# Moving the overflow loop of a mixture-of-experts sweep from its end to its middle

## The chip, the cores and the metric

One core of a Trainium2 chip runs the whole program. The metric is the device time of one execution in microseconds (us), a median over the runs of a kernel. The profile is one execution, taken by the hardware profiler.

## What is computed

A two-layer backbone over 512 latent tokens of width 1024, with 256 context tokens. Layer 0 mixes tokens with latent attention, layer 1 with a convolution module. After each mixer comes a mixture of experts (MoE) with 64 experts of hidden width 256, six chosen for each token, and one shared expert. All is in float32. Only the MoE matters here:

```
xs_pad = concat([xs, zeros((1, D))])
xg = xs_pad[slot_tok].reshape(n_blocks, 128, D)     # tokens grouped by expert, in blocks of 128 rows
yg = map(lambda xb, e: (silu(xb @ w1[e]) * (xb @ w3[e])) @ w2[e], (xg, blk_e))
routed = segment_sum(yg * slot_w, slot_tok)
out = routed + (silu(xs @ sh_w1) * (xs @ sh_w3)) @ sh_w2
```

How many tokens an expert gets depends on the routing. On this data most experts get 64 or fewer, some get 65 to 128, and in each layer one block of tokens lies beyond an expert's first 128.

## The kernel before

**The sweep.** `moe(i)` runs once for each layer. After routing, all engines sweep over experts u = 0 to 63, with the four blocks of the shared expert among the first ones. The w-th block of the sweep has place w; for u of 2 and more, `place(u) = u + 4`. For each expert TensorE (PE) runs `unit(u)`:

- `expert_in(u)`, the product with w1 and w3 ("up", bank 6). A flag in `big_i` picks one of two forms: `up_small` (L943, 32 matmuls, up to 64 tokens) or `up_mm` (L937, 16 matmuls). It first waits for the expert's weights (`w_in`) and its transposed rows (`xgT_ev`).
- `turn_rows(u+1)`: the next expert's gathered rows are transposed (L975, banks 1 and 2). VectorE (DVE) copies them out with `rows_out` (L1316).
- `down(u-1)`: the product of the expert before with w2 (L950 small, L964 large, banks 4 and 5).
- `turn_act(u)`: the activations are transposed (L970). DVE copies them out (L1322).

ScalarE (ACT) computes the SiLU of u (L583 small, L581 large; DVE multiplies, L1311 and L1309) and then `store(u-1)`. That copies the result out of PSUM (L609 or L607) into one of two buffers, `yb[0]` and `yb[1]`, and issues two DMAs to `y_rows` (L615). Before it overwrites a buffer it waits for that buffer's stores to land (`y_out`).

**The ring.** Weights lie in four slots of SBUF. SP, the engine that issues the weight loads, runs `refill_up` (L368, 2 MB: w1 and w3) when up has used a slot, and `refill_down` (L371, 1 MB: w2) when down has. One expert's weights are 3.15 MB, and SP keeps this order in its queue: up of u+1, then down of u.

**The rows.** GpSimd (POOL) gathers the rows of u+2 from `h_rows` by an indirect DMA (L467) as soon as the rows of u are transposed, into `xg[u % 2]`.

**The overflow loop.** Blocks beyond an expert's first 128 tokens are handled after expert 63, by a loop on every engine that runs `many` times, a count in `unit_i` that each engine loads into a register. Nothing in it overlaps: rows are gathered (L493), transposed, copied out (L1479), the up product (L937), SiLU (L652), product (L1481), transposition, copy (L1483), down product (L964), copy (L654), store of 512 KB (L656), and on ACT a wait for that store to land. Its weights go into the slot of expert 60, when expert 60's down product is done, with semaphore `t_w`.

**Combining.** When all stores have landed, POOL gathers the six results of each token (L509, 24 indirect DMAs) and DVE sums them (L1490). These lines begin it:

```
pool.wait_ge(y_out[s], 32 * E // 2 + i * 16 * E)      # for s in 0, 1
pool.wait_ge(m["dn_ps"], TT + E)
with nc.gpsimd.If(many > 0):
    pool.wait_ge(m["t_yout"], many * 16)
```

Of the kernel before, what the change touches and what calls it, by code (L numbers as in the profile page):

```python
# [26 lines left out]
E = 64  # L27
# [40 lines left out]
def build(nc, xT_d, ctxT_d, vec_d, cst_d, mod_w, wq_a, wq_b, wkv_a, wkv_b, wo, pw1, pw2,  # L68
# [10 lines left out]
    with ctx:  # L79
# [8 lines left out]
        def bank(b, n=1):  # L88
            return PS[:, b * 512:(b + n) * 512]
# [213 lines left out]
        def place(u):  # L303
            return u + 2 if u < 2 else u + 4

        def slot_of(u):
            return u if u < RING - 1 else (1, 3, 2, 0)[u % RING]

        def loads_of(u):
            return 1 if u < RING - 1 else (u - 5) // 4 + 1 if slot_of(u) == RING - 1 else (u - 2) // 4 + 1 if slot_of(u) == 2 \  # L310
                else (u - 3) // 4 + 2

# [32 lines left out]
        def _(sp):  # L345
# [12 lines left out]
            def load_moe(i):  # L358
# [34 lines left out]
                refill_up(5, RING - 1, SHARED_AT[3])  # L393
                with nc.sync.Fori(0, (E - 6) // 4) as g:
# [7 lines left out]
                sp.wait_ge(unit_rdy, i + 1)  # L402
                many = nc.sync.value_load(unit_i[0:1, XMAX:XMAX + 1], min_val=0, max_val=XMAX)
                with nc.sync.If(many > 0):
                    with nc.sync.Fori(0, many) as j:
                        sp.wait_ge(m["dn_ps"], TT + E - 3)
                        sp.wait_ge(m["t_dn"], j + 1)
                        e = nc.sync.value_load(unit_i[0:1, ds(j, 1)], min_val=0, max_val=E - 1)
                        expert(ds(e, 1), slot_of(E - 4), m["t_w"])

# [31 lines left out]
        def _(pool):  # L442
# [7 lines left out]
            def moe(i):  # L450
# [26 lines left out]
                gather(1, 1, xg_in[1])  # L477
                with nc.gpsimd.Fori(0, E // 2 - 1) as g:
# [3 lines left out]
                pool.wait_ge(xgT_ps, E - 1 + i * E)  # L482
# [52 lines left out]
        def _(a):  # L535
# [36 lines left out]
            def moe(i):  # L572
# [64 lines left out]
                shared_out(3)  # L637
                with nc.scalar.Fori(0, (E - 4) // 4) as g:
# [3 lines left out]
                either(E - 1, lambda big: silu(place(E - 1), 1, 1, big))  # L642
                either(E - 2, lambda big: store(E - 2, place(E - 2), 32 * ((E - 2) // 2), 0, big))
                either(E - 1, lambda big: store(E - 1, place(E - 1), 32 * ((E - 1) // 2), 1, big))
                a.sem_inc(m["t_yev"], 1)
                a.wait_ge(unit_rdy, i + 1)
                many = nc.scalar.value_load(unit_i[0:1, XMAX:XMAX + 1], min_val=0, max_val=XMAX)
                with nc.scalar.If(many > 0):
                    a.wait_ge(y_out[0], 32 * E // 2 + i * 16 * E)
                    with nc.scalar.Fori(0, many) as j:  # L650
# [7 lines left out]
                        a.wait_ge(m["t_yout"], j * 16 + 16)  # L658
                        A(tick[0:1, i:i + 1], zero[0:1, 0:1], ACT.Copy).then_inc(m["t_tick"], 1)

            a.wait_ge(x_in, 32)
# [104 lines left out]
        def _(pe):  # L766
# [166 lines left out]
            def moe(i):  # L933
# [166 lines left out]

                with nc.tensor.Fori(0, (E - 4) // 4) as g:
# [3 lines left out]
                unit(E - 1, slot_of(E - 1), slot_of(E - 2), 32 * loads_of(E - 1), None, 1)  # L1105
                either(E - 1, lambda big: down(place(E - 1), 1, slot_of(E - 1), big))

                many = nc.tensor.value_load(unit_i[0:1, XMAX:XMAX + 1], min_val=0, max_val=XMAX)
                with nc.tensor.If(many > 0):
                    with nc.tensor.Fori(0, many) as j:  # L1110
                        pe.wait_ge(m["t_xg"], j * 16 + 16)
                        rows_tr(0).then_inc(m["t_xgT_ps"], 1)
                        pe.wait_ge(m["t_xgT_ev"], j + 1)
                        pe.wait_ge(m["t_w"], j * 32 + 32)
                        up_mm(lambda c: xgT[0][:, c, :], slot_of(E - 4)).then_inc(m["t_up"], 1)
# [68 lines left out]
        def _(dve):  # L1184
# [114 lines left out]
            def moe(i):  # L1299
# [165 lines left out]
                weights()  # L1465
                with nc.vector.Fori(0, (E - 4) // 4) as g:
                    for r in range(4):
# [3 lines left out]
                        act_out(n, 1, (1 + r) % 2)  # L1471
                either(E - 1, lambda big: product(place(E - 1), 1, 1, big))
                act_out(place(E - 1), 1, 1)
                many = nc.vector.value_load(unit_i[0:1, XMAX:XMAX + 1], min_val=0, max_val=XMAX)
                with nc.vector.If(many > 0):
                    dve.wait_ge(m["up_ps"], TT + E - 1)
                    with nc.vector.Fori(0, many) as j:
# [3 lines left out]
                        V.tensor_tensor(act[0], gate[0], bank(6)[:, F:2 * F], ALU.mult).then_inc(m["t_act"], 1)  # L1481
                        dve.wait_ge(m["t_actT_ps"], j + 1)
                        V.tensor_copy(actT[0].rearrange("p k t -> p (k t)"), bank(7)[:, 0:F]).then_inc(m["t_actT_ev"], 1)  # L1483
                dve.wait_ge(m["y_ev"], SHARED_AT[3] + 1)
                for n in range(TT * K):
# [139 lines left out]
```

## Time and profile before

| | us |
|---|---|
| median of 3 runs | 2261.01 (2259.72 to 2262.26) |
| the profiled execution's own time | 2265.18 |
| its span, first to last instruction | 2263.4 |
| PE busy | 1923.2 (85%) |
| DVE, ACT, POOL busy | 829.7, 463.5, 346.2 |
| DMA | 624.04 MB, mean 276 GB/s |

Busy time is summed over instructions. Of PE it says little: matmuls are pipelined, and their ends are modelled. The sweep of layer 0 lies between about 584 us (up of expert 0) and 1184 us, that of layer 1 between about 1564 us and 2168 us.

### The profile page before, as it was taken

The page shows a single profiled execution, that of the slowest core. Times are in us where ns is not written, and L with a number is a line of the kernel's source. Part 1 is how long each engine was busy: PE and PEld are TensorE (multiplying, and loading weights), DVE is VectorE, ACT ScalarE, POOL GpSimd, SP SyncE. Part 2 cuts the span into 40 slices and gives each one's busy share as a digit, 9 for nine tenths or more (in the row PEclk, how much of TensorE's full clock was granted, in tenths as well). Part 3 has the DMA queues.
Part 4 walks back from the last instruction along what each step waited for, and adds up shares of the span by engine and source line. Part 5 has one row for each costly group of instructions (what it writes and reads, how often), then busy time and mean ns, then how long its engine had stood idle before and what let it go on. Part 6 is the DMA issues. An engine that isn't in the chain of part 4 may idle for free.

```text
span 2263.4 us, 30747 instructions
## 1 busy us (share of the span) xinstructions
PE 1923.2 (85%) x9400; PEld 990.9 (44%) x9401; DVE 829.7 (37%) x1481; ACT 463.5 (20%) x826; POOL 346.2 (15%) x538
## 2 busy tenths in 40 slices
PE   6999999899999878978891898788989789988952
PEld 3355555335444444444440443244444444444521
DVE  2237666405332222222225589435322212222225
ACT  4124344213011111111110455221111111110102
POOL 0000000000111111111104188001111111111122
PEclk8999999998999999999996899898999999999986
DMA  9697000567499999999987400035899999999954
GB/s 372 251 371 287 1 1 0 180 229 302 143 366 412 402 396 397 396 407 393 391 312 255 199 1 0 0 129 223 307 400 407 395 392 407 389 395 393 378 189 160
DMA packets 122815, 624.04 MB, mean 276 GB/s; under 512 B 18048, under 2 KB 19200, under 8 KB 87040
## 3 DMA queue, kind: packets, MB, share of 16 engines
q1 hardware_dynamic: 71776, 498.65, 55.8%
q0 software_dynamic: 26112, 79.72, 9.9%
q10 hardware_dynamic: 24864, 44.84, 5.6%
q8 instruction: 37, 0.61, 0.1%
q14 instruction: 26, 0.21, 0.0%
HBM read 562.34 MB, written 76.28 MB: 282 GB/s over the span
## 4 chain that ended last, share of the span: by engine, by line
PE 61%; DMA 22%; DVE 8%; issue 4%; POOL 2%; ACT 2%; SPq 0%; DVEq 0%; ACTq 0%; POOLq 0%
DMA ring<-in 19%; PE PS L937 10%; PE PS L943 9%; PE PS L1157 5%; PE PS L964 5%; PE PS L950 4%; PE PS L975 3%; PE PS L833 3%; PE PS L1175 3%; PE PS L928 2%; PE PS L862 2%; PE PS L794 2%; POOL work L509 2%; PE PS L918 2%; PE PS L785 2%
## 5 line engine op out<-in xcount | busy, mean ns | idle before, releaser
L943 PE MATMUL PS<-ring,work 128*64 128x256 f32 x3360 | 417.0, 405 | 111.1 <-issue 108.5
L943 PEld LDWEIGHTS PS<-ring,work 128*64 128x64 f32 x3360 | 248.1, 145 | 255.7 <-issue 160.6
L1311 DVE TENSOR_TENSOR work<-work,PS 64x256 f32<-64x256 f32 x105 | 44.4, 423 | 522.4 <-ACT work L583 519.2
L950 PE MATMUL PS<-ring,work 128*64 128x512 f32 x840 | 203.3, 605 | 1.4 <-ACT work L609 0.8
L937 PE MATMUL PS<-ring,work 128*128 128x512 f32 x400 | 182.3, 610 | 19.7 <-issue 13.4
L1316 DVE COPY work<-PS 128x1024 f32<-128x1024 f32 x128 | 156.7, 1224 | 14.8 <-PE PS L975 5.4
L461 POOL COPY col_i<-idx 128x1 int32 (+1 forms) x128 | 23.2, 181 | 848.9 <-PE PS L975 838.1
L467 POOL DMA_INDIRECT work<-h_rows,col_i x128 | 125.5, 981 | 169.4 <-issue 169.4
L975 PE MATMUL PS<-cst,work 128*128 128x128 f32 x1040 | 140.9, 278 | 0.6 <-DMA work<-h_rows,col_i 0.6
L583 ACT ACTIVATE work<-PS 64x256 f32<-64x256 f32 x105 | 39.4, 375 | 484.7 <-PE PS L943 484.7
L975 PEld LDWEIGHTS PS<-cst,work 128*128 128x128 f32 x1040 | 113.4, 141 | 54.2 <-issue 53.0
L937 PEld LDWEIGHTS PS<-ring,work 128*128 128x128 f32 x400 | 75.8, 195 | 110.7 <-issue 110.7
L1322 DVE COPY work<-PS 128x256 f32<-128x256 f32 x136 | 57.7, 424 | 178.3 <-PE PS L970 178.1
L964 PE MATMUL PS<-ring,work 128*128 128x512 f32 x264 | 119.2, 594 | 1.0 <-DVE work L1483 1.0
L1157 PE MATMUL PS<-hT,ring 128*128 128x512 f32 x256 | 113.3, 602 | 6.0 <-ACT hT L566 6.0
L609 ACT ACTIVATE work<-PS 128x512 f32<-128x512 f32 x105 | 62.7, 597 | 268.6 <-PE PS L950 236.0
L530 POOL TENSOR_TENSOR work<-work 128x512 f32<-128x512 f32 x80 | 104.8, 1313 | 76.5 <-ACT work L740 67.2
L881 PE MATMUL PS<-work,hT 96*128 96x512 f32 (+1 forms) x256 | 93.0, 486 | 0.0
L1127 PE MATMUL PS<-cst,work 128*128 128x128 f32 x64 | 12.2, 333 | 90.9 <-DVE work L1490 90.9
L454 POOL MEMSET work<- 128x1024 f32 x4 | 3.8, 980 | 554.4 <-DVE small L1371 554.4
L794 PE MATMUL PS<-sq,mean_w 128*128 128x512 f32 (+1 forms) x112 | 62.2, 672 | 28.4 <-ACT sq L550 25.3
L950 PEld LDWEIGHTS PS<-ring,work 128*64 128x64 f32 x840 | 51.2, 136 | 79.5 <-issue 77.5
(226 smaller groups left out, 2230.9 us busy)
## 6 DMA issues: line engine op xcount, KB each, us to landing
ring<-in SPq DMA_DIRECT2D x156, 2048.0 KB, 17.4
ring<-in SPq DMA_DIRECT2D x130, 1024.0 KB, 17.8
y_rows<-zrow POOLq DMA_DIRECT2D x2, 14336.0 KB, 70.8
y_rows<-work ACTq DMA_DIRECT2D x210, 128.0 KB, 9.1
ring<-in SPq DMA_DIRECT2D x3, 4096.0 KB, 27.5
y_rows<-work ACTq DMA_DIRECT2D x46, 256.0 KB, 9.9
ring<-in SPq DMA_DIRECT2D x1, 8192.0 KB, 25.1
ring<-in SPq DMA_DIRECT2D x2, 3072.0 KB, 12.3
```

Source lines behind the costliest of these rows:

```text
L467: pool.indirect_dma_start(out=xg[n][0:p], out_offset=None, in_=h_rows[i], in_offset=bass.IndirectOffsetOnAxis(ap=col_i[0:p, n:n + 1], axis=0),
L530: nc.gpsimd.tensor_tensor(side[c % 2], before, tap_prod[n % 4], ALU.add).then_inc(side_add, 1)
L794: mm(bank(NB)[:, 0:w], mean_w[:, :], sq[:, c % 2, 0:w], start=(c == 0), stop=(c == DC - 1)).then_inc(sq_used, 1)
L833: last = mm(bank(4 + g % 4)[0:M_, 0:w], lhs, hA[:, c, c0:c0 + w], start=(c == 0), stop=(c == DC - 1))
L881: last = mm(bank(2 * (n % 2), 2)[:, c0:c0 + w], qT[m % 2][q][0:96, t * 128:(t + 1) * 128], kT[m % 2][q][0:96, c0:c0 + w], start=True, stop ...
L937: last = mm(bank(6), lhs(c), w13(s)[:, :, c, :], start=(c == 0), stop=(c == DC - 1))
L943: last = mm(bank(6)[64 * q:64 * q + 64, 0:F], lhs(c)[:, 0:64], w13(s)[:, q, c, :], start=(c == 0), stop=(c == DC - 1), tile_position=(0, 6 ...
L950: last = mm(bank(4)[64 * q:64 * q + 64, :], actT[par][:, kk, 0:64], w2(s)[:, kk, q * 512:(q + 1) * 512], start=(kk == 0), stop=(kk == 1), ...
L964: last = mm(bank(4 + half), actT[par][:, kk, :], w2(s)[:, kk, half * 512:(half + 1) * 512], start=(kk == 0), stop=(kk == 1))
L975: last = tr(bank(1, 2)[:, c * 128:(c + 1) * 128], xg[par][:, c * 128:(c + 1) * 128], ident)
L1157: last = mm(bank(2 * (c % 2) + half), pw1_sb[:, kk, half * D + c * 128:half * D + (c + 1) * 128], hM[:, kk, :], start=(kk == 0), stop=(kk ...
L1316: V.tensor_copy(xgT[par].rearrange("p c t -> p (c t)"), bank(1, 2)).then_inc(xgT_ev, 1)
```

## The change

The overflow loop now stands between experts 38 (`MID`) and 39 on every engine.

- **Ring.** The overflow block takes one turn of the ring, as if it were an expert of its own: it gets slot 0, which expert 35 used, and each later expert the slot one turn further on. `RING_TURN`, `turn_of` and `slot_of` say so.
- **SP.** Both loads of the overflow block are issued when the down product of 35 is done, after a load of `many` and one of the expert's number. They stand ahead of the loads of 39. The refill of 42 (slot 0) waits for the overflow block's down product; behind it in SP's queue are the up load of 43 and the down load of 42.
- **POOL.** The overflow rows are gathered after the rows of 38 are transposed, and the gathers of 40 and on wait until the overflow rows are transposed.
- **PE.** The down product of 38 is no longer overlapped with the up product of 39 but comes before the overflow block. After the block PE waits for ACT's copy of its result (`t_yev`), and the unit of 39 has no down product in it.
- **ACT.** The loop first waits for the stores of `yb[0]` through expert 38 to land, then takes the SiLU. It ends in the wait for the overflow block's own store, as before; now the SiLU of 39 comes behind it.
- **DVE.** One wait is added (`dn_ps`, before the copy into `actT[0]`).
- At the end of the sweep the overflow loop is gone. The waits at the head of combining are the same.

```diff
-            return u if u < RING - 1 else (1, 3, 2, 0)[u % RING]
+            return u if u < RING - 1 else RING_TURN[turn_of(u) % RING]
...
-                for u in range((E - 6) // 4 * 4 + 5, E):
+                for u in range((MID - 6) // 4 * 4 + 5, MID + 1):
+                    if u < MID:
+                        refill_up(u + 1, slot_of(u + 1), u + 1)
+                    refill_down(u, slot_of(u), u)
+                sp.wait_ge(unit_rdy, i + 1)
+                sp.wait_ge(m["dn_ps"], place(MID - 3) + 1)
+                many = nc.sync.value_load(unit_i[0:1, XMAX:XMAX + 1], min_val=0, max_val=XMAX)
+                with nc.sync.If(many > 0):
+                    with nc.sync.Fori(0, many) as j:
+                        sp.wait_ge(m["t_dn"], j + 1)
+                        e = nc.sync.value_load(unit_i[0:1, ds(j, 1)], min_val=0, max_val=E - 1)
+                        expert(ds(e, 1), EXTRA_SLOT, m["t_w"])
+                for u in range(MID + 1, MID + 4):
+                    refill_up(u, slot_of(u), place(u - 3))
+                    refill_down(u, slot_of(u), place(u - 3))
+                with nc.sync.If(many > 0):
+                    sp.wait_ge(m["t_dn"], many + 1)
+                    sp.sem_inc(m["t_tick"], 1)
+                refill_up(MID + 4, slot_of(MID + 4), place(MID - 3))
+                refill_up(MID + 5, slot_of(MID + 5), MID + 5)
+                refill_down(MID + 4, slot_of(MID + 4), place(MID - 3))
...
+                    pool.wait_ge(m["t_xgT_ps"], many + 1)
+                    nc.gpsimd.tensor_tensor(tick[0:1, 8 * i + 5:8 * i + 6], zero[0:1, 0:1], zero[0:1, 0:1], ALU.add)
+                with nc.gpsimd.Fori(0, (E - MID - 2) // 2) as g:
+                    for r in range(2):
+                        pool.wait_ge(xgT_ps, g * 2 + (MID + 1 + r) + i * E)
+                        gather(g * 2 + (MID + 2 + r), r, xg_in[r])
...
-                    a.wait_ge(y_out[0], 32 * E // 2 + i * 16 * E)
+                    a.wait_ge(y_out[0], 32 * (MID // 2 + 1) + i * 16 * E)
...
+                either(MID, lambda big: down(place(MID), 0, slot_of(MID), big))
 
                 many = nc.tensor.value_load(unit_i[0:1, XMAX:XMAX + 1], min_val=0, max_val=XMAX)
                 with nc.tensor.If(many > 0):
+                    pe.wait_ge(xgT_ev, MID + 2 + i * E)
...
-                        pe.wait_ge(m["y_ev"], TT + E)
-                        down_mm(0, slot_of(E - 4)).then_inc(m["t_dn"], 1)
+                        pe.wait_ge(m["y_ev"], place(MID) + 1)
+                        down_mm(0, EXTRA_SLOT).then_inc(m["t_dn"], 1)
+                    pe.wait_ge(m["t_yev"], many + 1)
+
+                expert_in(MID + 1, place(MID + 1), slot_of(MID + 1), 32 * loads_of(MID + 1), 1)
+                turn_rows(MID + 2, 16 * ((MID + 2) // 2 + 1), 0)
+                turn_act(place(MID + 1), 1)
...
+                        dve.wait_ge(m["dn_ps"], place(MID) + 1)
```

The rest of the diff splits each engine's loop over experts in two, up to `MID` and from `MID + 1`, with the few units between them written out.

## Rows read from the trace of the kernel before

**Rows 1.** Stretches of time: busy us by engine, granted clock, DMA share, GB/s.

```profile
960.00:1100.00 140.00, 113.56 (x766) 60.65 (x764) 33.14 (x48) 15.25 (x32) 21.43 (x48) 0.95 1.02 400
...
1150.00:1185.00 35.00, 34.26 (x219) 18.12 (x218) 9.02 (x14) 5.61 (x10) 4.19 (x10) 1.00 0.84 299
...
1900.00:1950.00 50.00, 49.41 (x219) 25.14 (x219) 10.22 (x15) 6.17 (x10) 6.80 (x15) 1.00 1.01 396
...
1970.00:2000.00 30.00, 29.21 (x175) 15.53 (x176) 7.82 (x11) 3.73 (x7) 4.36 (x11) 0.99 0.98 378
```

**Rows 2.** Groups of PE, 964 to 1101 us: busy, mean ns, idle before.

```profile
L943 PE MATMUL PS<-ring,work 128*64 128x256 f32 x480 | 61.8, 416 | 24.5 <-issue 24.5
...
L937 PE MATMUL PS<-ring,work 128*128 128x512 f32 x1 | 1.2, 1214 | 2.4 <-issue 2.4
```

**Rows 3.** The same, 1956 to 2077 us.

```profile
L943 PE MATMUL PS<-ring,work 128*64 128x256 f32 x384 | 49.1, 414 | 14.8 <-issue 14.8
...
L937 PE MATMUL PS<-ring,work 128*128 128x512 f32 x17 | 10.0, 744 | 5.0 <-issue 5.0
```

**Rows 4.** Timeline at layer 0's end: start us, us, engine line op.

```profile
1184.22 1.09 PE L975 MATMUL PS<-cst,work 128*128 128x128 f32 x8
...
1185.36 1.12 ACTq L615 DMA_DIRECT2D y_rows<-work  x2
...
1186.72 7.13 PE L937 MATMUL PS<-ring,work 128*128 128x512 f32 x16 [1.40 <-DVE work L1479]
...
1193.89 0.38 ACT L652 ACTIVATE work<-PS 128x256 f32<-128x256 f32 x1 [8.56 <-PE PS L937]
...
1195.73 3.70 PE L964 MATMUL PS<-ring,work 128*128 128x512 f32 x8 [0.52 <-DVE work L1483]
...
1200.68 0.36 ACTq L656 DMA_DIRECT2D y_rows<-work  x1
...
1203.73 0.95 POOL L509 DMA_INDIRECT work<-y_rows,row_i  x1
```

**Rows 5.** Stores, issue to landing: L615 at the end of layer 0 (1185 to 1188 us).

```profile
DMA to landing us min/median/max: 2.3/2.3/2.4
```

**Rows 6.** The same of L656, both its executions.

```profile
DMA to landing us min/median/max: 2.6/2.6/2.7
```

**Rows 7.** Timeline at layer 1's end.

```profile
2168.77 1.14 ACTq L615 DMA_DIRECT2D y_rows<-work  x2
...
2187.35 0.96 POOL L509 DMA_INDIRECT work<-y_rows,row_i  x1
```

**Rows 8.** L368, the overflow block's 2 MB load (issued at 1169.5 us).

```profile
DMA to landing us min/median/max: 8.9/8.9/8.9
```

**Rows 9.** SP's timeline, layer 1: up load of 39, down load of 39.

```profile
1906.40 0.33 SPq L368 DMA_DIRECT2D ring<-in  x1
...
1921.20 0.33 SPq L371 DMA_DIRECT2D ring<-in  x1
```

**Rows 10.** SP's register load ahead of the overflow block's loads, ns.

```profile
L408 SPq TENSOR_LOAD <-unit_i x2: 274/278/283, 1168.8 to 2152.5; - x2
```

**Rows 11.** L371, the 1 MB load of 38 in layer 1 (issued at 1909.14 us).

```profile
DMA to landing us min/median/max: 16.1/16.1/16.1
```

**Rows 12.** PE's timeline around expert 39, layer 1.

```profile
1939.07 0.44 PE L970 MATMUL PS<-cst,work 128*128 128x128 f32 x2
...
1948.12 3.67 PE L943 MATMUL PS<-ring,work 128*64 128x256 f32 x32
```

**Rows 13.** Stores of L615, issue to landing, 1940 to 1990 us.

```profile
DMA to landing us min/median/max: 7.5/10.5/13.6
```

**Rows 14.** L371, the 1 MB load of 38 in layer 0 (issued at 929.66 us).

```profile
DMA to landing us min/median/max: 15.8/15.8/15.8
```

**Rows 15.** Stores of L615, issue to landing, 930 to 990 us.

```profile
DMA to landing us min/median/max: 8.3/10.2/13.7
```

**Rows 16.** The page's DMA issues: gathers of rows, median us to landing.

```profile
work<-h_rows,col_i POOLq DMA_INDIRECT x130, 8.9
```

More of the change, by code:

```diff
@@ L304, in place, with turn_of @@
             return u + 2 if u < 2 else u + 4
+        MID = 38
+        RING_TURN = (0, 1, 3, 2)
+        def turn_of(u):
+            return u - 3 if u <= MID else u - 2
         def slot_of(u):
-            return u if u < RING - 1 else (1, 3, 2, 0)[u % RING]
+            return u if u < RING - 1 else RING_TURN[turn_of(u) % RING]
         def loads_of(u):
-            return 1 if u < RING - 1 else (u - 5) // 4 + 1 if slot_of(u) == RING - 1 else (u - 2) // 4 + 1 if slot_of(u) == 2 \
-                else (u - 3) // 4 + 2
+            return sum(slot_of(x) == slot_of(u) for x in range(u + 1))
+        EXTRA_SLOT = RING_TURN[(MID - 2) % RING]
+        assert EXTRA_SLOT == slot_of(MID - 3)
         ROW_BANK = [n % 2 for n in range(4)] + [3, 0] * 4 + [(2, 4, 5, 6)[n % 4] for n in range(12)]
@@ L397, in load_moe @@
                         refill_down(g * 4 + (5 + r), slot_of(5 + r), g * 4 + (5 + r))
[L398 removed]
+                for u in range((MID - 6) // 4 * 4 + 5, MID + 1):
[19 more added lines that the diff above has]
+                refill_down(MID + 4, slot_of(MID + 4), place(MID - 3))
+                with nc.sync.Fori(0, (E - MID - 6) // 4) as g:
+                    for r in range(4):
+                        refill_up(g * 4 + (MID + 6 + r), slot_of(MID + 6 + r), g * 4 + (MID + 6 + r))
+                        refill_down(g * 4 + (MID + 5 + r), slot_of(MID + 5 + r), g * 4 + (MID + 5 + r))
+                for u in range((E - MID - 6) // 4 * 4 + MID + 5, E):
                     if u + 1 < E:
@@ L659, in moe @@
                         A(tick[0:1, i:i + 1], zero[0:1, 0:1], ACT.Copy).then_inc(m["t_tick"], 1)
+                either(MID + 1, lambda big: silu(place(MID + 1), 1, 1, big))
+                for u in range(MID + 2, MID + 5):
+                    either(u, lambda big: silu(place(u), 1, u % 2, big))
+                    either(u - 1, lambda big: store(u - 1, place(u - 1), 32 * ((u - 1) // 2), (u - 1) % 2, big))
+                with nc.scalar.Fori(0, (E - MID - 5) // 4) as g:
+                    for r in range(4):
+                        u = MID + 5 + r
+                        either(g * 4 + u, lambda big: silu(g * 4 + place(u), 1, u % 2, big))
+                        either(g * 4 + (u - 1), lambda big: store(g * 4 + (u - 1), g * 4 + place(u - 1), g * 64 + 32 * ((u - 1) // 2), (u - 1) % 2, big))
+                either(E - 1, lambda big: silu(place(E - 1), 1, 1, big))
+                either(E - 2, lambda big: store(E - 2, place(E - 2), 32 * ((E - 2) // 2), 0, big))
+                either(E - 1, lambda big: store(E - 1, place(E - 1), 32 * ((E - 1) // 2), 1, big))
             a.wait_ge(x_in, 32)
@@ L1119, in moe @@
                         pe.wait_ge(m["t_yev"], j + 1)
-                        pe.wait_ge(m["y_ev"], TT + E)
-                        down_mm(0, slot_of(E - 4)).then_inc(m["t_dn"], 1)
+                        pe.wait_ge(m["y_ev"], place(MID) + 1)
[4 more added lines that the diff above has]
+                turn_act(place(MID + 1), 1)
+                for u in range(MID + 2, MID + 5):
+                    unit(u, slot_of(u), slot_of(u - 1), 32 * loads_of(u), 16 * ((u + 1) // 2 + 1), u % 2)
+                with nc.tensor.Fori(0, (E - MID - 5) // 4) as g:
+                    for r in range(4):
+                        u = MID + 5 + r
+                        unit(g * 4 + u, slot_of(u), slot_of(u - 1), g * 32 + 32 * loads_of(u), g * 32 + 16 * ((u + 1) // 2 + 1), u % 2)
+                unit(E - 1, slot_of(E - 1), slot_of(E - 2), 32 * loads_of(E - 1), None, 1)
+                either(E - 1, lambda big: down(place(E - 1), 1, slot_of(E - 1), big))
                 pe.wait_ge(comb_used, TT * K + i * TT * K)
@@ L1482, in moe @@
                         dve.wait_ge(m["t_actT_ps"], j + 1)
+                        dve.wait_ge(m["dn_ps"], place(MID) + 1)
                         V.tensor_copy(actT[0].rearrange("p k t -> p (k t)"), bank(7)[:, 0:F]).then_inc(m["t_actT_ev"], 1)
+                for u in range(MID + 1, MID + 5):
+                    either(u, lambda big: product(place(u), 1, u % 2, big))
+                    rows_out(u + 1, (u + 1) % 2, u + 4)
+                    act_out(place(u), 1, u % 2)
+                with nc.vector.Fori(0, (E - MID - 5) // 4) as g:
+                    for r in range(4):
+                        u = MID + 5 + r
+                        either(g * 4 + u, lambda big: product(g * 4 + place(u), 1, u % 2, big))
+                        rows_out(g * 4 + (u + 1), (u + 1) % 2, g * 4 + (u + 4))
+                        act_out(g * 4 + place(u), 1, u % 2)
+                either(E - 1, lambda big: product(place(E - 1), 1, 1, big))
+                act_out(place(E - 1), 1, 1)
                 dve.wait_ge(m["y_ev"], SHARED_AT[3] + 1)
```

32 lines of the change are left out of this document (9 added, 23 removed).

## The prediction

> **What bounds the kernel now.** I read the stretches of time first. In the sweeps the DMA engines are busy all the time and move about 400 GB/s: in layer 0 from 960 to 1100 us, that is from expert 40 to 54, and in layer 1 even from 1900 to 1950 us, where PE is busy 99% of the time too [rows 1]. The groups of PE say the same: in layer 0 PE sat idle 24.5 + 2.4 us ahead of up products, and in layer 1, from 1956 us on, 14.8 + 5.0 us [rows 2, 3]. The releaser is called "issue", because the wait for weights stands in PE's sequencer. So the second half of a sweep costs its bytes at 0.4 MB/us, down to the last ten experts, where PE is the bound: DMA 0.84, 299 GB/s, and PE 34.3 of 35 us [rows 1].
>
> Then the timeline of a layer's end. The overflow block starts at 1184.22 us, alone, and its up product's last wait is for a DVE copy, not for weights. The first combining gather leaves at 1203.73 us [rows 4]. The reader is to see two resources: at the end the block costs latency and no bandwidth, in the middle bandwidth and perhaps latency.
>
> **What leaves the end.** Without the block, combining waits for the stores of expert 63. They are issued at 1185.36 us and half a us later, and land 2.3 to 2.4 us on: 1188.3 [rows 4, 5]. Now the block's store leaves at 1200.68 and lands 2.6 later at 1203.3, and the gather follows 0.4 after that [rows 4, 6]. With the same 0.4, combining starts at 1188.7, 15.05 us earlier. In layer 1 the stores leave at 2168.77 and half a us later, land at about 2171.7, and the gather goes from 2187.35 to 2172.1, 15.25 us earlier [rows 7]. Gain: **30.3 us**. The work on PE, ACT and DVE that stood there is the same work in the middle. DVE's added wait costs nothing: it counts down(38), which PE does ahead of the block.
>
> **What the middle pays in bytes.** The block brings 3.15 MB of weights, a store of 0.52 MB and few gathered rows, some 0.1 MB: 3.77 MB. At 0.4 MB/us that is 9.4 us a layer, **18.9 us** in all. At the end these bytes were free. Here nothing covers them, DMA being busy behind [rows 1]. Bounds: the weights alone, 7.9 a layer, and the 9.4.
>
> **What it pays in holes.** When DMA runs dry, that time is lost as well. The trace of before doesn't have the new order, so I lay it out from rows. A quiet 2 MB load lands after 8.9 us [rows 8]. Its bytes take 5.2; of the other 3.7 I put 2 ahead of the first byte.
>
> *Layer 1, first hole.* SP used to send the up load of 39 at 1906.40, when up(35) was done. That slot now goes to the block, whose loads leave only after down(35), at 1921.2 [rows 9], and after two register loads of 0.28 with their register work [rows 10], some 1.2 by my estimate: 1922.4, first byte 1924.4. The last load ahead of it, the down load of 38, landed at 1925.2 [rows 11]. Without the 2.1 MB of 39 beside it, it lands 5.2 earlier, at 1920. A hole of 4.4; a store fills some: 4. Bounds 2 and 5.
>
> *Layer 1, second hole.* From 1924.4 DMA has the weights of the block, 39, 40 and 41 (12.6 MB), and stores and gathers (1.9 MB): dry at 1961. The refill of 42 waits for the block's down product. PE ends down(37) and the transposition at 1939.5 [rows 12]. Down(38) was hidden behind up(39) before; now it waits some 1.2 for DVE's copy and takes 3.6: 1944.3. Transposition and copy 2.5 (1184.22 to 1186.72), up 7.1 [rows 4]: 1954. ACT's SiLU, though, waits for the store of 38. It leaves at about 1946.2 and takes 10.5 under load [rows 13]: 1956.7, so the SiLU is 2.7 late. From the SiLU to the end of down is 5.5 (1193.89 to 1199.4 [rows 4]): 1962.3. The refill's first byte is there at 1964.4. Hole 3.3. Bounds 0.6 and 6.
>
> *Layer 1, third hole.* The block's store leaves at 1963.6, and on ACT the SiLU of 39 is queued behind its landing. Behind that SiLU stand DVE's product, DVE's `rows_out` of 40, PE's `turn_act(39)` and up(40), then SP's load of 44, which waits for up(40). The landing takes between 2.6 (quiet) and 10.5 (loaded) [rows 6, 13], so up(40) ends between 1973.5 and 1980. DMA has 5.8 MB (42, the up load of 43, the store) until 1979. The hole is 0 to 3.2, and I take 1.5, DMA being half quiet then. Against the three stand 1.6 us that DMA missed before from 1970 to 2000 us (378 GB/s for 400 [rows 1]) and needn't miss again. Layer 1: 4 + 3.3 + 1.5 - 1.6 = **7.2 us**.
>
> *Layer 0.* The down load of 38, sent at 929.66, landed at 945.5 [rows 14], without 39's bytes at 940.3. Down(35) ended at about 936.3, so the block's first byte is there at 939.5: no hole. By the steps above (the store of 38 in flight for 10.2 us [rows 15]) the block's down product ends at 971.5, and DMA is fed until 975. Up(40) ends at 989, its load of 44 arrives at 991, and DMA is dry at 989.8: **1.2 us**. Bounds 0 and 6. What makes the layers differ is that in layer 1 large experts come just ahead of 38: slots are freed late, and SP's backlog is shorter.
>
> *PE* pays more than DMA: about 20 us in layer 0, and 27 in layer 1 (up(40) at 1975 for 1948.12 [rows 12]). It wins the difference to DMA's shift back out of its idle time behind: 20 - 10.6 of 26.9 us, and 27 - 16.6 of 19.8 us [rows 2, 3]. POOL's order costs nothing: from the block's transposed rows to those of 40 PE has up, down and up(39), over 18 us, to cover the gather of 40 (8.9 to land [rows 16]).
>
> **Sum.** -30.3 + 18.9 + 7.2 + 1.2 = -3.0. It is made on the profiled execution, 2265.2 us by its own time, of which the span is 2263.4. That execution lies 4.2 us, 0.2%, over the median of the runs. I take the difference off the median: 2261.0 - 3.0 = **2258.0**.
>
> A rule speaks against the third hole. By the Trainium skill, "DMA: Bandwidth & Descriptors", "Queues, rings and completion order", each DMA engine takes turns between the queues that have work, so that ACT's store needn't wait out SP's backlog. With the same page's fit ("Anatomy of one DMA", 2.0 us and the bytes at 436 GB/s) the block's store lands after an estimated 3.2 us. The trace so far doesn't agree: in the sweep at most half as many bytes took 7.5 to 13.7 us [rows 13, 15].
>
> **The rivals.**
>
> *DMA stays fed.* SP's backlog covers every hole. For it: DMA's share never fell from 1900 to 1950 us. Against it: that was with the load of 39 sent 15 us earlier. Time: -30.3 + 18.9 = -11.4, 2249.6. Chance 0.25.
>
> *Stores land fast.* If they land in the middle as at the end, in 2.6 us, the block's SiLU isn't late, layer 1's second hole shrinks to 0.6, and its third and layer 0's go: 4 + 0.6 - 1.6 = 3.0, in all -8.4, 2252.6. For it: the queue is ACT's own. Against it: rows 13 and 15. Chance 0.1. The skill's rule above would come out here.
>
> *ACT's two waits for stores, slower.* If the landings behind which the two SiLUs stand take 13.2 us each, near the maxima of 13.6 and 13.7 [rows 13, 15], that is 2.7 more each. The second hole grows by 2.7 and the third by 4.2 in layer 1, and layer 0 loses 5.4 more: +12.3, 2270.3. For it: one store is twice as large as any in those rows. Against it: DMA is less loaded just then. It decides from the point where holes sum to 11.4 us, for 8.4 in the forecast. Chance 0.2.
>
> *PE doesn't win its delay back.* The clock was 0.95 before where PE idled [rows 1]. If idling in the block brings the low clock oftener, so that layer 1 keeps 22 of its 27 us, that is 5.4 more: 2263.4, to 2268 if layer 0 does the same. Chance 0.05.
>
> **How the numbers follow.** The forecast has the other 0.4, with its own range 2253 to 2264 by the bounds of the holes. 0.2% is 4.5 us, about what a measurement of this kernel can tell. Of the forecast 0.28 lie within that, 0.1 below and 0.02 above. The two fast rivals give 0.29 faster and 0.06 same, the third 0.17 slower and 0.03 same, the last 0.05 slower. That makes faster 0.39, same 0.37, slower 0.24. The range is 2248 (no hole, and a little less than the bytes) to 2269 (just short of the third rival, whose upper half is left out).
>
> **What would show it.** Combining starts some 3.4 us after ACT's last copy. DMA's rate dips two or three times within 60 us of up(38) in layer 1, and hardly in layer 0. L656 takes 5 to 11 us to land, and the SiLU of 39 starts right behind it. The up product of expert 63 comes 10.6 us later in layer 0 and 16.6 us in layer 1, against the start of its sweep. The forecast is wrong if these are off by over 3 us in sum, above all if the first hole of layer 1 isn't there.

## The result, and the profile after

Slower. The changed kernel takes 2278.07 us (median of 6 runs, 2267.59 to 2283.08), the kernel before in the same runs 2261.64: a ratio of 1.0068 (95% interval 1.0047 to 1.0090). The forecast was 2258.0 with a range of 2248 to 2269, so the time lies outside it, on the side of the third rival.

The first lines of the page of the changed kernel. Its profiled execution took 2267.59 us by its own time, the shortest of its runs; that of before lay 4.2 us over its median.

```profile
span 2265.5 us, 30598 instructions
...
PE 1919.8 (85%) x9400; PEld 988.9 (44%) x9401; DVE 829.3 (37%) x1481; ACT 463.9 (20%) x826; POOL 344.9 (15%) x540
...
DMA packets 122832, 624.27 MB, mean 276 GB/s; under 512 B 18048, under 2 KB 19200, under 8 KB 87040
```

Work and bytes are nearly the same. What moved is time without work, and two places tell most of it.

**The end.** The timeline of the changed kernel at the end of layer 1: the up product of expert 63, its store, the first combining gather.

```profile
2177.59 3.67 PE L984 MATMUL PS<-ring,work 128*64 128x256 f32 x32
...
2186.47 1.12 ACTq L646 DMA_DIRECT2D y_rows<-work  x2
2190.42 0.96 POOL L540 DMA_INDIRECT work<-y_rows,row_i  x1 [0.50 <-issue]
```

From that product to the gather there are 12.8 us, in layer 0 too. Before there were 27.9 and 27.6. The gain at the end is 15.1 + 14.8 = 29.9 us, for 30.3 in the forecast.

**The middle.** The stretches of the changed kernel (columns as in [rows 1]), in layer 0 and in layer 1.

```profile
950.00:960.00 10.00, 8.22 (x24) 3.82 (x24) 1.23 (x1) 0.60 (x1) 2.88 (x7) 1.00 1.03 422
960.00:970.00 10.00, 4.68 (x16) 2.04 (x18) 0.85 (x2) 1.41 (x2) 0.00 (x0) 1.00 0.97 344
970.00:980.00 10.00, 4.16 (x38) 2.67 (x34) 0.00 (x0) 0.47 (x2) 1.34 (x3) 0.94 1.01 397
980.00:990.00 10.00, 7.91 (x48) 4.44 (x50) 3.54 (x5) 0.48 (x2) 0.37 (x2) 0.72 0.61 188
...
1910.00:1920.00 10.00, 10.00 (x57) 5.52 (x56) 3.49 (x5) 1.40 (x2) 1.83 (x6) 1.00 0.57 196
1920.00:1930.00 10.00, 10.00 (x33) 4.91 (x33) 0.93 (x3) 1.41 (x2) 1.04 (x1) 1.00 1.00 408
...
1940.00:1950.00 10.00, 5.69 (x14) 2.23 (x12) 0.00 (x0) 0.00 (x0) 1.60 (x4) 0.91 1.03 413
1950.00:1960.00 10.00, 6.18 (x10) 2.51 (x10) 0.85 (x2) 0.38 (x1) 0.00 (x0) 0.58 0.20 83
1960.00:1970.00 10.00, 4.79 (x41) 3.07 (x40) 0.00 (x0) 1.02 (x1) 1.20 (x3) 1.00 0.89 328
1970.00:1980.00 10.00, 6.58 (x35) 3.53 (x35) 1.98 (x3) 0.58 (x2) 0.21 (x1) 0.66 0.67 283
1980.00:1990.00 10.00, 10.00 (x70) 5.24 (x69) 3.72 (x5) 1.49 (x4) 1.82 (x6) 1.00 0.89 327
```

Where DMA moved about 400 GB/s without a break [rows 1], layer 1 now has three dips, and the one in the middle, 83 GB/s, is all but empty. Layer 0 has one large dip, at 980 us (and 303 and 343 GB/s from 920 to 940). While DMA is nearly empty from 1950 to 1960, PE is not the bound either: it is without work until 1953.3, and its granted clock is 0.58. The timeline of that place in layer 1 says on what it all hangs:

```profile
1915.70 0.36 SPq L376 DMA_DIRECT2D ring<-in  x1
1916.26 0.52 SPq L379 DMA_DIRECT2D ring<-in  x1
...
1932.58 3.70 PE L1005 MATMUL PS<-ring,work 128*128 128x512 f32 x8 [0.52 <-DVE work L1377]
...
1937.43 0.87 ACTq L646 DMA_DIRECT2D y_rows<-work  x2
...
1938.56 7.13 PE L978 MATMUL PS<-ring,work 128*128 128x512 f32 x16 [1.40 <-DVE work L1532]
...
1952.41 0.38 ACT L681 ACTIVATE work<-PS 128x256 f32<-128x256 f32 x1 [15.01 <-DMA y_rows<-work]
...
1953.30 0.69 PE L1011 MATMUL PS<-cst,work 128*128 128x128 f32 x2 [7.61 <-DVE work L1534]
...
1954.51 5.59 PE L1005 MATMUL PS<-ring,work 128*128 128x512 f32 x8 [0.52 <-DVE work L1537]
...
1960.20 6.48 SPq L376 DMA_DIRECT2D ring<-in  x2
1961.33 0.37 ACTq L685 DMA_DIRECT2D y_rows<-work  x1
1962.64 3.67 PE L984 MATMUL PS<-ring,work 128*64 128x256 f32 x32 [2.54 <-issue]
...
1970.92 0.38 ACT L614 ACTIVATE work<-PS 64x256 f32<-64x256 f32 x1 [0.72 <-issue]
...
1971.81 0.55 PE L1011 MATMUL PS<-cst,work 128*128 128x128 f32 x2 [4.47 <-DVE work L1366]
```

Read it as one chain. The up product of the block ends at 1945.7. Its SiLU (L681) waits until 1952.4, because ACT first wants the store of expert 38, sent at 1937.4, to have landed: about 14.5 us, by the end of the wait. The down product (L1005) comes after 7.6 us of idling and takes 5.59 us for the 3.70 of the same eight matmuls at 1932.58. Only then may SP refill slot 0 (1960.20), and 43 and the rest are queued behind it. Then the block's store takes its time:

```profile
DMA to landing us min/median/max: 8.6/8.6/8.6
```

(L685 in layer 1; 10.5 in layer 0.) The SiLU of 39 (L614) stands behind it, and PE waits 4.5 us again.

From the up product of expert 3 to that of 63 before took 541.5 us in layer 0 and 548.7 in layer 1. The changed kernel takes 556.6 and 571.4: 15.1 and 22.7 us more, for 10.6 and 16.6 in the forecast. The table below calls this measure "3 to 63".

### The profile page after: what moved, and what is told of

Its sections match the earlier page's. It is cut to its first block, busy times and chain, and to the rows that moved or that the text cites. A ratio compares the mean times of both kernels' runs of the same rounds, so it can differ in the third digit from the quotient of the medians.

```text
span 2265.5 us, 30598 instructions
## 1 busy us (share of the span) xinstructions
PE 1919.8 (85%) x9400; PEld 988.9 (44%) x9401; DVE 829.3 (37%) x1481; ACT 463.9 (20%) x826; POOL 344.9 (15%) x540
## 4 chain that ended last, share of the span: by engine, by line
PE 61%; DMA 20%; DVE 8%; issue 5%; POOL 2%; ACT 2%; SPq 1%; ACTq 0%; DVEq 0%; POOLq 0%
DMA ring<-in 16%; PE PS L984 11%; PE PS L978 9%; PE PS L991 5%; PE PS L1212 5%; PE PS L1005 5%; PE PS L1016 4%; DMA y_rows<-work 3%; PE PS L874 3%; PE PS L1230 3%; PE PS L969 2%; PE PS L903 2%; PE PS L959 2%; POOL work L540 2%; PE PS L922 2%
## 5 line engine op out<-in xcount | busy, mean ns | idle before, releaser
L978 PE MATMUL PS<-ring,work 128*128 128x512 f32 x400 | 177.6, 597 | 14.8 <-issue 9.6
L486 POOL COPY col_i<-idx 128x1 int32 (+1 forms) x128 | 23.4, 183 | 837.3 <-PE PS L1016 828.2
L1016 PEld LDWEIGHTS PS<-cst,work 128*128 128x128 f32 x1040 | 113.4, 141 | 54.9 <-issue 51.9
L614 ACT ACTIVATE work<-PS 64x256 f32<-64x256 f32 x105 | 39.5, 376 | 470.2 <-PE PS L984 466.5
L1005 PE MATMUL PS<-ring,work 128*128 128x512 f32 x264 | 121.2, 602 | 1.5 <-DVE work L1537 1.0
L1182 PE MATMUL PS<-cst,work 128*128 128x128 f32 x64 | 12.5, 338 | 91.8 <-DVE work L1556 91.8
L1011 PEld LDWEIGHTS PS<-cst,work 128*128 128x128 f32 x276 | 30.3, 141 | 124.6 <-issue 95.5
## 6 DMA issues: line engine op xcount, KB each, us to landing
ring<-in SPq DMA_DIRECT2D x2, 3072.0 KB, 12.5
```

Source lines behind the costliest of these rows:

```text
L978: last = mm(bank(6), lhs(c), w13(s)[:, :, c, :], start=(c == 0), stop=(c == DC - 1))
L1005: last = mm(bank(4 + half), actT[par][:, kk, :], w2(s)[:, kk, half * 512:(half + 1) * 512], start=(kk == 0), stop=(kk == 1))
L1016: last = tr(bank(1, 2)[:, c * 128:(c + 1) * 128], xg[par][:, c * 128:(c + 1) * 128], ident)
```

## The experiments

All ratios are to the kernel before, run beside them on the same chip. Runs on different chips are compared by their ratios, where 0.001 is 2.3 us. "3 to 63" comes from the one profiled execution of each, and two executions of one kernel differ there by 3.3 us (first two rows, layer 0). A ratio and the quotient of two medians differ by up to 0.0006, well within the intervals. Where PE's rate is read, TensorE's granted clock of a stretch is the share of full speed (2.4 GHz), so 0.5 is 1.2 GHz.

| run | us | ratio (95%) | 3 to 63, layer 0 / 1 |
|---|---|---|---|
| changed kernel | 2278.07 | 1.0068 (1.0047 to 1.0090) | 556.6 / 571.4 |
| after_again | 2278.53 | 1.0065 (1.0042 to 1.0089) | 559.9 / 571.8 |
| no_block | 2233.16 | 0.9858 (0.9835 to 0.9881) | 541.4 / 547.8 |
| act_late | 2260.09 | 0.9989 (0.9974 to 1.0003) | 553.0 / 562.3 |
| both | 2260.21 | 0.9986 (0.9968 to 1.0004) | 554.9 / 562.3 |
| no_weights | 2274.74 | 1.0048 (1.0029 to 1.0067) | 559.2 / 567.3 |
| early_load | 2278.65 | 1.0066 (1.0039 to 1.0094) | 564.0 / 568.8 |
| overlap | 2255.57 | 0.9974 (0.9953 to 0.9995) | 553.8 / 555.9 |
| overlap_26 | 2251.82 | 0.9957 (0.9939 to 0.9976) | 554.2 / 555.4 |
| silu_block | 2266.01 | 1.0022 (1.0008 to 1.0037) | 555.4 / 564.4 |
| silu_39 | 2267.51 | 1.0036 (1.0018 to 1.0053) | 560.1 / 572.6 |
| mid_26 | 2271.92 | 1.0046 (1.0031 to 1.0061) | 557.7 / 564.5 |
| split_no_block | 2237.72 | 0.9893 (0.9874 to 0.9913) | 545.4 / 551.7 |

**after_again** is the changed kernel once more, **no_block** the kernel before with a block count of zero, so that the overflow block's work is left out altogether.

```diff
-                V.tensor_copy(unit_i[0:1, XMAX:XMAX + 1], bank(0)[0:1, 128:129]).then_inc(unit_rdy, 1)
+                V.memset(unit_i[0:1, XMAX:XMAX + 1], 0).then_inc(unit_rdy, 1)
```

> The changed kernel itself, timed beside the next three. In its profile both sweeps are longer (last up product against the up product of expert 3, 15.1 us in layer 0 and 22.7 us in layer 1) and both ends shorter (14.8 and 15.0 us), which makes 8 us. Expected: 8 to 15 us slower than before, and in the profile again DMA dips right behind expert 39.

> The kernel before with the count of overflow blocks set to 0, so that the block's work is left out altogether. It measures what the block costs at the end. If the end is worth what the profiles say, it is 29 to 31 us faster than before: the whole loss is then in the middle (30 and the 8 to 15 us that the changed kernel is slower). Rival, that part of the gain at the end is illusory since combining starts into busier DMA queues: less than 26 us.

The slowdown repeats. Without the block the kernel before is 30.7 us faster (2263.84 us beside it, 2233.16 without), the gather starts 13.1 and 13.0 us after the up product of 63, and the sweeps take as long as with it. So the block cost its end and nothing else, and that is what the change gets back. All that follows is about the middle.

**act_late** makes ACT wait for the stores of `yb[0]` only where it is about to overwrite `yb[0]`: the wait for the store of 38 goes from ahead of the block's SiLU to ahead of its copy, and the wait for the block's store from ahead of the SiLU of 39 to the copy of 40. **both** adds an early load: SP issues the block's 2 MB when the up product of 35 is done, not its down product.

```diff
-                    a.wait_ge(y_out[0], 32 * (MID // 2 + 1) + i * 16 * E)
+                    a.sem_inc(m["t_yout"], 16)
                     with nc.scalar.Fori(0, many) as j:
                         a.wait_ge(m["t_up"], j + 1)
                         A(gate[0], bank(6)[:, 0:F], ACT.Silu).then_inc(m["t_gate"], 1)
+                        a.wait_ge(y_out[0], 32 * (MID // 2 + 1) + i * 16 * E)
+                        a.wait_ge(m["t_yout"], j * 16 + 16)
...
-                        a.wait_ge(m["t_yout"], j * 16 + 16)
-                        A(tick[0:1, i:i + 1], zero[0:1, 0:1], ACT.Copy).then_inc(m["t_tick"], 1)
...
+                    if u == MID + 3:
+                        with nc.scalar.If(many > 0):
+                            a.wait_ge(m["t_yout"], many * 16 + 16)
+                            A(tick[0:1, i:i + 1], zero[0:1, 0:1], ACT.Copy).then_inc(m["t_tick"], 1)
```

The early load, on SP:

```diff
+                            sp.wait_ge(m["up_ps"], place(MID - 3) + 1)
+                            expert_up(ds(e0, 1), EXTRA_SLOT, m["t_w"])
                     refill_down(u, slot_of(u), u)
...
+                    sp.wait_ge(m["dn_ps"], place(MID - 3) + 1)
+                    expert_down(ds(e0, 1), EXTRA_SLOT, m["t_w"])
```

> The changed kernel, but ACT waits for the stores of yb[0] only where it overwrites yb[0]: no longer ahead of the block's SiLU, and not ahead of the SiLU of expert 39. In the changed kernel's profile these waits made the SiLUs 1.5 and 6.6 us late in layer 0, 6.7 and 4.7 us late in layer 1, 19.5 us. If they keep SP's refills and so DMA waiting, most of it comes back: 12 to 19 us faster than the changed kernel, at or below the time before. If PE had time to make up for it anyway, so that only bytes count: within 4 us of the changed kernel.

> act_late, and SP sends the block's 2 MB load as soon as the up product of expert 35 is done, ahead of the down load of 38, as it would for any expert. If the first hole of layer 1 (DMA at 196 GB/s from 1910 to 1920 us, 5 us lost) is real loss: 4 to 6 us less than act_late, in all 6 to 12 us under the time before. If a sweep is bound by PE there: the same as act_late.

The two waits cost 18.4 us (2278.53 to 2260.09). Without them the change is worth nothing that can be measured: the ratio 0.9989 is 2.5 us, and its interval reaches past 1. The early load adds nothing, where 4 to 6 us were expected if the first hole was real loss. The timeline of act_late in layer 1, the chain from above:

```profile
1938.57 7.13 PE L982 MATMUL PS<-ring,work 128*128 128x512 f32 x16 [1.40 <-DVE work L1536]
1945.73 0.38 ACT L681 ACTIVATE work<-PS 128x256 f32<-128x256 f32 x1 [8.38 <-PE PS L982]
...
1947.58 3.70 PE L1009 MATMUL PS<-ring,work 128*128 128x512 f32 x8 [0.52 <-DVE work L1541]
1951.38 9.25 SPq L376 DMA_DIRECT2D ring<-in  x2
1952.40 1.02 ACT L685 ACTIVATE work<-PS 128x1024 f32<-128x1024 f32 x1 [6.28 <-DMA y_rows<-work]
```

The SiLU comes 6.7 us earlier, the down product has its 3.70 us back, and the refill leaves 8.8 us earlier for the same start of the block. The wait now stands ahead of the copy (L685), where it costs about 1 us. Now the stretches of act_late, and below them those of both:

```profile
1910.00:1920.00 10.00, 10.00 (x57) 5.51 (x56) 3.49 (x5) 1.40 (x2) 1.83 (x6) 1.00 0.53 184
...
1950.00:1960.00 10.00, 6.37 (x35) 3.23 (x34) 0.00 (x0) 1.02 (x1) 0.00 (x0) 0.83 0.94 337
```

```profile
1910.00:1920.00 10.00, 10.00 (x43) 5.16 (x43) 2.03 (x3) 1.41 (x2) 1.33 (x3) 1.00 0.81 323
...
1950.00:1960.00 10.00, 6.19 (x21) 2.71 (x22) 0.85 (x2) 1.41 (x2) 0.00 (x0) 0.93 0.48 167
```

The early load fills the first dip (184 to 323 GB/s), and the second one opens by as much (337 to 167). With the three stretches between, 17.6 MB were moved from 1910 to 1960 us in the one and 17.1 in the other. That gave a theory of its own. From the down product of 35 to that of the block DMA may load the weights of the block, 39, 40 and 41, 12.6 MB, and nothing else, because all other slots are in use. Whoever starts them earlier has them sooner and then waits for the same product. I call it the slots.

**no_weights** tests it from the other side. It is the changed kernel without the loads of the block's weights: the block is computed with what lies in the slot. If bytes are the price, 6.3 MB give back 16 us. **early_load** is the early load alone.

```diff
-                        expert(ds(e, 1), EXTRA_SLOT, m["t_w"])
+                        sp.sem_inc(m["t_w"], 32)
```

> The changed kernel without the load of the block's weights (SP adds to the semaphore instead, and the block computes with the weights of expert 35 that lie in the slot); 3.15 MB less for DMA in each layer. Bytes theory (the forecast's): 7.9 us less in each layer, some 16 us faster than the changed kernel. Slot theory (new): the refill of 42 and all behind it wait for the block's down product, and until then DMA can only load 39 to 41, whatever else it had to do; so the last up product moves by less than 2 us in each layer, and the whole stays within 4 us of the changed kernel, slower than before.

> The changed kernel with one edit: SP sends the block's 2 MB load when up(35) is done, ahead of the down load of 38. Forecast's theory of holes that add up: the first hole of layer 1 goes, 4 to 5 us faster than the changed kernel. Slot theory: DMA fills the first hole and runs dry that much earlier ahead of the refill of 42; less than 1.5 us gained, and the second hole is deeper.

Leaving the weights out gives 4 us, not 16: the ratio goes from 1.0065 to 1.0048. The early load gives nothing here either (1.0066). Two stretches of no_weights in layer 1, whose sweep began some 10 us later, so that they stand beside 1910 to 1920 and 1950 to 1960 of the changed kernel (196 and 83 GB/s):

```profile
1920.00:1930.00 10.00, 10.00 (x60) 5.88 (x59) 3.42 (x5) 1.74 (x3) 1.46 (x4) 1.00 0.53 181
...
1960.00:1970.00 10.00, 7.08 (x14) 3.02 (x16) 0.33 (x1) 1.02 (x1) 0.00 (x0) 0.67 0.26 79
```

Most of the bytes that were left out came back as empty time. Over the 90 us around the block DMA moved 308 GB/s in layer 0 (910 to 1000 us), for 358 in the changed kernel and 347 in after_again: 20.7 us missing at 400 GB/s, for 9.5 and 11.9. In layer 1 it moved 294 (1910 to 2000), for 312 in the changed kernel (1900 to 1990): 23.9 missing, for 19.8. What layer 1 did gain, 4 us in 3 to 63, is not from bytes directly: the store of 38 landed in about 10 us instead of 14.5 (first half sent at 1947.94, SiLU at 1958.28), and the refill of 42 left 350.1 us after the up product of 3 instead of 354.0.

One rival fits these runs as well as the slots do: that only PE's own delay counts, and DMA's holes don't. The trace of the changed kernel speaks against it. From 400 to 500 us after the up product of 3, PE again idles ahead of up products with releaser "issue", as in [rows 2]: 17.6 us in layer 0 and 12.6 in layer 1, for 15.2 and 12.5 in the same stretches before. So PE had caught up with the weights, and they set the pace again.

**overlap** shortens PE's path and touches no byte. To both it adds that the block's rows are transposed ahead of the down product of 38, so that their copy is hidden behind it, and that PE waits for the copy of the block's result ahead of the down product of 39, no longer ahead of its up product. **overlap_26** is the same with `MID = 26`.

```diff
-                either(MID, lambda big: down(place(MID), 0, slot_of(MID), big))
                 many = nc.tensor.value_load(unit_i[0:1, XMAX:XMAX + 1], min_val=0, max_val=XMAX)
                 with nc.tensor.If(many > 0):
                     pe.wait_ge(xgT_ev, MID + 2 + i * E)
-                    with nc.tensor.Fori(0, many) as j:
-                        pe.wait_ge(m["t_xg"], j * 16 + 16)
-                        rows_tr(0).then_inc(m["t_xgT_ps"], 1)
+                    pe.wait_ge(m["t_xg"], 16)
+                    rows_tr(0).then_inc(m["t_xgT_ps"], 1)
+                either(MID, lambda big: down(place(MID), 0, slot_of(MID), big))
...
-                    pe.wait_ge(m["t_yev"], many + 1)
...
                 turn_act(place(MID + 1), 1)
+                with nc.tensor.If(many > 0):
+                    pe.wait_ge(m["t_yev"], many + 1)
```

> both, and on PE the block's rows are transposed ahead of down(38), so that down(38) covers DVE's copies, and the wait for ACT's copy of the block's result stands ahead of down(39), no longer ahead of up(39). PE reaches the block's down product some 2 us earlier and up(39) some 4.5 us earlier. Slot theory: sweeps 2 to 4.5 us shorter each than in act_late, in all 5 to 8 us under it, 2252 to 2256 us, below the time before. Bytes theory (act_late is already at the bytes): within 2 us of act_late.

> overlap with MID = 26, where four small experts come ahead of the block in both layers (in layer 1 ahead of 38 stand two large ones, and 38 is large). PE takes some 5 us less from down(MID - 3) to the block's down product in layer 1. Slot theory: layer 1's sweep another 2 to 5 us shorter than in overlap, layer 0's the same. Bytes theory: no difference.

Both are faster than the kernel before, the second by 0.43%, 9.9 us. The timeline of overlap in layer 1 shows the down product of the block, the up product of 39 directly behind it, and that of 40:

```profile
1947.50 3.70 PE L1016 MATMUL PS<-ring,work 128*128 128x512 f32 x8 [0.52 <-DVE work L1552]
1951.13 3.67 PE L995 MATMUL PS<-ring,work 128*64 128x256 f32 x32
1951.30 3.87 SPq L376 DMA_DIRECT2D ring<-in  x2
...
1958.71 3.67 PE L995 MATMUL PS<-ring,work 128*64 128x256 f32 x32 [1.85 <-issue]
```

And its lowest stretches in that layer:

```profile
1910.00:1920.00 10.00, 10.00 (x57) 5.51 (x56) 2.03 (x3) 1.51 (x3) 1.33 (x3) 1.00 0.78 296
...
1950.00:1960.00 10.00, 7.55 (x57) 4.38 (x57) 1.98 (x3) 1.40 (x2) 1.40 (x3) 1.00 0.87 321
```

The same bytes, and no empty stretch. Against both, the ratio falls from 0.9986 to 0.9974, 2.7 us, by less than the intervals; in the profile layer 1 gains 6.4 us and layer 0 gains 1.1. Expected were 5 to 8 us under act_late; by the ratios it is 3.4, and in layer 0 nothing (553.8 for 553.0). The sweeps are 12.3 and 7.2 us longer than before, 19.5 in all, next to the 18.9 us of the bytes alone. That the sums agree may be chance, as the bytes are 9.4 in each layer. Of overlap_26, layer 1 was expected another 2 to 5 us shorter and is 0.5 shorter in the profile (555.4 for 555.9). By the ratios it is 3.8 us faster than overlap, within the intervals, so that the place 26 helps here isn't shown.

**silu_block** moves only the first of ACT's two waits, **silu_39** only the second; **mid_26** sets only `MID = 26`; **split_no_block** is the changed kernel with a block count of zero, the block's work left out.

> The changed kernel with the first of act_late's two edits: the wait for the stores of expert 38 stands behind the block's SiLU. The wait for the block's own store ahead of the SiLU of 39 stays. Slot theory: the block's down product, and with it the refill of 42, comes 1.6 us earlier in layer 0 and 6.7 us in layer 1, so 5 to 9 us faster than the changed kernel, nearly all of it in layer 1. If the two waits only work together (PE catching up otherwise): under 3 us.

> The changed kernel with the second edit alone: the wait for the block's store is put off to the store of 40. The refill of 42 is as late as in the changed kernel, but up(40), and with it the load of 44, comes 5 to 7 us earlier in both layers. Slot theory: 4 to 10 us faster, in both layers, layer 0 more than from the first edit. Together with silu_block about the 18 us of act_late.

> The changed kernel with MID = 26 for 38, nothing else. Four small experts stand ahead of the block in both layers. Slot theory: layer 1's sweep 4 to 7 us shorter than with 38, layer 0's the same. If 38 is as good a place as any: within 2 us in both.

> The changed kernel with the count of overflow blocks set to 0, so that the block's work is left out altogether, in the changed order of code. It should take what no_block takes, 2233 us within 3: then the split loops and units written out cost nothing by themselves. If they do cost, by instruction loading or by branches, it is over 3 us slower than no_block, and that much of the loss is not the block's.

By the ratios, from 1.0065, the first wait costs 9.7 us, the second 6.6, and together (1.0065 to 0.9989) 17.2: within the intervals of some 4 us they add up. The profiled execution of silu_39 was 9.5 us over its own median, so its 3 to 63 says nothing. Moving the block to 26 gives 4.3 us by the ratios, within the uncertainty (1.0031 to 1.0061 beside 1.0042 to 1.0089). In the profiles the gain is in layer 1 (571.4 to 564.5), where large experts stand ahead of 38; in layer 0 there is none.

Split_no_block was expected within 3 us of no_block. It is 7.9 us slower by the ratios, and 4.0 and 3.9 us by 3 to 63. The reordered code costs that, with no block in it. What fits is the ring: slot 0 waits unused from 35 to 42, DMA dips to 277 and 215 GB/s from 1900 to 1920 us (and to 322, 323 and 267 from 920 to 950), and the down product of 38 isn't overlapped. But the changed program also loads more instructions by DMA (1.05 MB in all for 0.82), and no run tells the two apart.

## Why the prediction was wrong

**What leaves the end** was right: 29.9 us for 30.3, and no_block confirms it.

**What the middle pays in bytes** named a true number in the wrong place. The 3.77 MB a layer are moved, and overlap shows 19.5 us beside 18.9, perhaps by chance (12.3 and 7.2 for 9.4 and 9.4). But in the changed kernel they were not what was paid: without 84% of them it wins 4 us. Bytes and holes were added as if independent. With the slots as the bound, bytes left out become a longer hole, as no_weights shows.

**What it pays in holes** is the step that failed. The forecast put the holes, less what is won back, at 8.4 us; they came to 19.0 (29.5, less 10.5). The two waits in front of ACT's SiLUs are what made most of it: act_late takes 18.4 us away by moving them. The terms, with the holes measured as what the stretches miss of 400 GB/s from 910 to 990 and from 1900 to 1990 us (with 343 GB/s from 1900 to 1910, 391 from 910 to 920, 429 from 940 to 950 and 422 from 1930 to 1940 beside the rows shown; before, the same stretches miss 0.2 and 1.7):

| us | forecast, layer 0 / 1 | measured |
|---|---|---|
| bytes | 9.4 / 9.4 | 9.4 / 9.4 |
| holes | 1.2 / 8.8 | 9.6 / 19.9 |
| won back | 0 / -1.6 | -3.9 / -6.6 (what is left over) |
| 3 to 63 | 10.6 / 16.6 | 15.1 / 22.7 |

- *Layer 1, first hole*: forecast 4. The two stretches from 1900 miss 1.4 + 5.1. It is where it was said to be, but early_load (285 GB/s in its lowest 10 us there, 1925.5 to 1935.5) and both (323) fill more than half of it and gain nothing: by itself it was no loss.
- *Layer 1, second hole*: forecast 3.3, bounds 0.6 and 6. It is about 10 (1950 to 1970 miss 7.9 + 1.8). Counted from the up product of 3 (at 1606.2 us, before at 1610.7), the refill of 42 left 2.4 us later than forecast and DMA ran dry some 5 us earlier (at about 1951.7). Earlier, because the block's loads left 2.2 us earlier and the bytes went at 0.408 MB/us (1917 to 1951), not at 0.4; that makes some 3 of the 5, and the rest isn't accounted for. Later, because the down product ran at the low clock, 1.9 us more. The SiLU itself came when forecast, at 346.2 us for 346.0: the store of 38 took 4 us longer than the 10.5 (about 14.5, over every row of [rows 13]), but had left 4.2 us earlier, with the block's up product 3.7 earlier. So the wait was 6.7 us for 2.7 in the forecast without making the chain later than forecast. What was misjudged is that this chain, against the bytes that the slots allow, sets the hole: in act_late, without the wait and with the product at full clock, the refill left 8.8 us earlier.
- *Layer 1, third hole*: forecast 1.5, with 3.2 as its upper bound. 1970 to 1990 miss 2.9 + 1.8 = 4.7. The landing of 8.6 us lay within the forecast's 2.6 to 10.5, and the SiLU of 39 was 4.7 late.
- *Layer 0*: forecast 1.2 with a bound of 6. 920 to 940 miss 3.9, where I had said "no hole", and 980 to 990 misses 5.3. The block's store took 10.5 us, the SiLU of 39 was 6.6 late, and behind it the load of 44. "Hardly in layer 0" was wrong. The dip from 920 to 940 stands in split_no_block too (322 and 323 GB/s), so the block's work doesn't make it.

**PE** was forecast late by 20 and 27 us at the up product of 40; it was 23.4 and 30.4. It won back 8.3 and 7.7 us, for the 9.4 and 10.4 of the forecast. So it was off by 3.4 us a layer at the block and by 1 to 3 behind it. The low clock, which the forecast priced only in its last rival, is part of that in layer 1, 1.9 us on the block's down product. Right behind ACT's second wait the up product of 40 took 6.05 us in layer 1 and 5.02 in layer 0, for 3.67 at full clock; that is as large as the 1 to 3, but no run tests it.

**The rivals.** *ACT's two waits, slower* was the right mechanism, and act_late shows it: without them the change gives 2.5 us, close to the 3.0 of the forecast. Its price was too small. I gave it 12.3 us over the forecast, with each landing at 13.2. The landings were 14.5 and 8.6 in layer 1, 23.1 together for its 26.4, so longer landings don't explain the difference. That the low clock and the slots do is argued, not shown. *DMA stays fed* (2249.6) is what overlap_26 nearly reaches (2251.82), but by other edits. *PE doesn't win its delay back* named 22 us kept in layer 1, and 22.7 were kept. That is luck: its ground was that PE would win back 5 us, and PE won back 7.7, of a delay of 30.4 and not 27. *Stores land fast* did not happen. The block's store took 7.6 to 12.1 us, the least in act_late and the most in overlap_26. The rule of the Trainium skill ("DMA: Bandwidth & Descriptors", "Queues, rings and completion order"), turns between the queues, thus doesn't give the landing of a whole store, and the estimate of 3.2 us from the fit in "Anatomy of one DMA", which that section gives for DMAs issued by GpSimd, is far too low here.

**What stays open.** The sweeps and ends add up to 37.8 - 29.9 = 7.9 us for the changed kernel and to 41.5 - 29.9 = 11.6 for after_again. The profiled executions as a whole differ from that of before by 2.4 and 10.7 us, and the medians by 16.4 and 14.7. The profiled execution of before was 4.2 us over its median, and the two others 10.5 and 2.7 under theirs. So 8.5 us of the timed difference of the changed kernel, and 3.1 of after_again's, have no place in their profiles, and the account above is of the profiled part alone. Also open: why DMA was faster in the rest of the changed sweep (403 GB/s against 393 from 2010 to 2120 us), and what a fifth slot would give, which wasn't tried. The slots themselves are argued from no_weights, early_load and both; no run changed their number. That the two waits cost the 18 us is shown, by act_late and its halves.

## What to carry to other kernels

Moving serial work from an uncovered end into a bandwidth-bound middle pays only if the middle's prefetch doesn't hang on that work: count the bytes that free buffers allow, and compare their time with the latency of the chain that frees the next one. If the chain is longer, shorten the chain (two waits put off to where the buffer is overwritten gave 18 us, and with two overlaps on PE and another place in the sweep the change became worth 9.9). Earlier loads gave nothing here, and 6.3 MB fewer bytes gave 4 us of 16. Bytes and holes are then one cost, not two terms of a sum.

## What the runs showed of the hardware

- How long a store takes under load does not follow from its size. 512 KB took 2.6 us at the end of a sweep [rows 6] and 8.6 and 10.5 in the middle; two halves of 256 KB each took about 14.5 us, behind DMA at 422 and 413 GB/s, and about 10 in no_weights.
- In layer 1 PE was without work for 7.6 us, did a short transposition, waited 0.5 us, and then took 5.59 us for the eight matmuls that take 3.70 at full clock. The granted clock was 1.00 until 1948, 0.53 from there to 1950, 0.50 (1.2 GHz) until 1957 and 0.78 from there to 1960. In no_weights, after 2.9 us idle and the same transposition, they took 6.06; in layer 0 of the changed kernel, after 2.3 us, they took 3.70.
- Behind the dips at 930 and 1915 us DMA moved 408 to 429 GB/s for some 20 to 30 us, behind those at 985 and 1975 us 399 to 406. The kernel before reached 420 and 429 in single stretches without any dip (980 to 990 and 1890 to 1900), so that DMA is faster after a hole isn't shown.
